# The sum of squares of the first norm: from eight TensorE products to GpSimd adds, with ScalarE's squares moved behind its rounding

## The reference, cut to what matters

```python
def rms_norm(x, g):
    xf = x.astype(jnp.float32)
    y = xf * lax.rsqrt(jnp.mean(xf * xf, axis=-1, keepdims=True) + EPS)
    return (y * g.astype(jnp.float32)).astype(x.dtype)

def diff_attention_layer(x, norm_g, w_in, ...):
    h = rms_norm(x, norm_g)
    q, k, v, z = jnp.split(h @ w_in, 4, axis=-1)
    q = rms_norm(q.reshape(b, s, DA_HEADS, 2, DA_HEAD), q_norm_g) * (DA_HEAD ** -0.5)
    ...
    return x + o @ w_out
```

## Time and profile before

| | |
|---|---|
| median of 3 runs | 1898.15 us (1897.22 to 1900.37) |
| span of the profiled execution, first to last instruction | 1896.2 us |
| TensorE products busy | 1868.0 us, 99% of the span |
| VectorE / ScalarE / GpSimd busy | 53% / 43% / 7% |
| mean granted TensorE clock | 0.998 of full speed |

### The profile page before, as it was taken

The page is one execution under the profiler, slowest core; times in us unless marked ns, Lnnn a source line. Parts: engine busy times, 40 slices in busy tenths (PEclk is TensorE's granted clock), DMA queues, the critical chain, the costliest instruction groups (busy, mean ns, idle before and its releaser), DMA issues.

```text
span 1896.2 us, 22387 instructions
## 1 busy us (share of the span) xinstructions
PE 1868.0 (99%) x8923; PEld 1450.5 (76%) x8923; DVE 996.8 (53%) x1778; ACT 817.9 (43%) x1328; POOL 123.8 (7%) x148
## 2 busy tenths in 40 slices
PE   8999999999999999999999999999999999999997
PEld 6566666666788788888886777778888878888886
DVE  6667666666544653333346667845434763333322
ACT  6566656656633342222323655434432442222221
POOL 0111111110001000000010011000000100000000
PEclk9999999999999999999999999999999999999999
DMA  5444343432233232222333323221123323233331
GB/s 199 164 145 156 144 145 145 145 145 101 78 129 117 67 111 100 93 96 94 100 86 125 99 70 106 68 94 35 45 89 111 124 92 102 94 100 97 92 95 61
DMA packets 56526, 201.95 MB, mean 107 GB/s; under 512 B 6478, under 2 KB 6934, under 8 KB 55784
## 3 DMA queue, kind: packets, MB, share of 16 engines
q1 hardware_dynamic: 44616, 158.32, 25.3%
q0 software_dynamic: 11808, 42.21, 6.1%
HBM read 195.23 MB, written 5.28 MB: 106 GB/s over the span
## 4 chain that ended last, share of the span: by engine, by line
PE 87%; DVE 6%; ACT 4%; issue 1%; DMA 0%; SPq 0%; DVEq 0%; ACTq 0%
PE ps L1204 25%; PE ps L1207 24%; PE ps L1205 24%; PE ps L1304 2%; PE ps L1268 2%; PE ps L1340 1%; ACT wH L1910 1%; PE ps L1292 1%; DVE wL L1499 1%; PE ps L1280 1%; ACT a L2009 1%; DVE a L1622 1%; PE ps L1347 1%; PE ps L1257 1%; DVE g1a L1499 1%
## 5 line engine op out<-in xcount | busy, mean ns | idle before, releaser
L1204 PE MATMUL ps<-hH,wH 128*128 128x512 f32 (+1 forms) x1560 | 634.8, 407 | 1.0 <-DVE hL L1570 1.0
L1207 PE MATMUL ps<-hH,wL 128*128 128x512 f32 (+1 forms) x1560 | 610.7, 391 | 1.0 <-DVE wL L1499 0.7
L1205 PE MATMUL ps<-hL,wH 128*128 128x512 f32 (+1 forms) x1560 | 609.0, 390 | 0.0
L1499 DVE TENSOR_TENSOR wL<-wr,wH 128x1024 fp32r<-128x1024 f32 (+2 forms) x285 | 343.9, 1207 | 483.8 <-ACT wH L1910 483.2
L1910 ACT ACTIVATE wH<-wr 128x1024 fp32r<-128x1024 f32 (+2 forms) x285 | 295.1, 1036 | 233.3 <-PE ps L1207 218.3
L1204 PEld LDWEIGHTS ps<-hH,wH 128*128 128x128 f32 (+1 forms) x1560 | 292.7, 188 | 93.6 <-issue 32.4
L1207 PEld LDWEIGHTS ps<-hH,wL 128*128 128x128 f32 (+1 forms) x1560 | 292.3, 187 | 66.9 <-DVE wL L1499 3.9
L1205 PEld LDWEIGHTS ps<-hL,wH 128*128 128x128 f32 (+1 forms) x1560 | 293.1, 188 | 61.3 <-issue 6.5
L1204 PE MATMUL ps<-gffn,wH 128*128 128x512 f32 x400 | 157.0, 393 | 1.0 <-DVE xT L1677 0.9
L1205 PE MATMUL ps<-gffn,wH 128*128 128x512 f32 x400 | 155.8, 390 | 0.0
L1207 PE MATMUL ps<-gffn,wL 128*128 128x512 f32 x400 | 155.8, 390 | 0.0
(11 more groups left out here) (304 smaller groups left out, 2079.9 us busy)
## 6 DMA issues: line engine op xcount, KB each, us to landing
wr<-wst SPq DMA_DIRECT2D x268, 512.0 KB, 3.4
a<-wfd POOLq DMA_DIRECT2D x54, 512.0 KB, 5.0
xT<-wfd POOLq DMA_DIRECT2D x18, 512.0 KB, 6.9
wr<-wst SPq DMA_DIRECT2D x16, 384.0 KB, 3.0
xT<-xin SPq DMA_DIRECT2D x8, 256.0 KB, 6.8
xT<-xin SPq DMA_DIRECT2D x2, 1024.0 KB, 7.0
xsave<-xT SPq DMA_DIRECT2D x1, 2048.0 KB, 7.3
c<-wfd POOLq DMA_DIRECT2D x8, 256.0 KB, 3.7
```

What stands on the lines that cost most here:

```text
L1204: e.matmul(o, hi, xh[k], start=k == 0, stop=False)
L1205: e.matmul(o, hi, xl[k], start=False, stop=False)
L1207: i = e.matmul(o, lo, xh[k], start=False, stop=k == t.nk - 1)
L1499: e.tensor_tensor(dst, x, hi.bitcast(F32), ALU.subtract).then_inc(s[name], 1)
```

## The change

Only the norm of x at the start is touched. The squares of x now go the way of the other norms: GpSimd adds chunks 0 to 6 into a buffer that nothing else uses at that time (`Vn[0]`), and TensorE sums two operands. The steps of the start are put in another order: all eight raw steps come first, with weight split 0 behind the first; then split 1; squares 0 to 3; split 2; squares 4 to 6; and square 7, at which TensorE does its two sums, stands between the fourth and the fifth chunk product of tv. Squares 4 to 7 wait for the add that has read their buffer.

```diff
-        self.add("norm_rs", n=n, stat=8 + 2 * n, rs=rs)
+        self.add("norm_rs", n=n, stat=2 + 2 * n, rs=rs)
...
         d.update(n=n, c=c, nsq=self.sig("nsq"))
-        if n == 0:
-            free = ("stat", self.sig("stat"))
-            d["stats"] = [free[1]]
-        elif c == 7:
+        if c == 7:
...
-        def chunk(c):
-            self.raw(0, c)
-            free[c % 4] = self.square(0, c, v=("first", c % 4), free=free[c % 4])
+        def square(c):
+            free[c % 4] = self.square(0, c, v=("first", c % 4), free=free[c % 4], acc_free=("rs", 0))
...
-        chunk(0)
-        chunk(1)
+        self.raw(0, 0)
         self.add("split", j=0)
-        mm(tq, 0, 1)
-        chunk(2)
-        chunk(3)
+        for c in range(1, 8):
+            self.raw(0, c)
+        mm(tq, *range(8))
         self.add("split", j=1)
-        mm(tq, 2, 3)
-        for c in range(4, 8):
-            chunk(c)
+        for c in range(4):
+            square(c)
         self.add("split", j=2)
-        mm(tq, 4, 5, 6, 7)
         mm(tk, *range(8))
-        mm(tv, *range(8))
+        for c in range(4, 7):
+            square(c)
+        mm(tv, 0, 1, 2, 3)
+        square(7)
+        mm(tv, 4, 5, 6, 7)
         rs = self.sig("rs")
-        self.add("norm_rs", n=0, stat=8, rs=rs)
+        self.add("norm_rs", n=0, stat=2, rs=rs)
...
-            return {1: acc1, 2: ff[0]["tmp"][0], 3: tq[0], 4: ff[1]["tmp"][0]}[n]
+            return {0: Vn[0], 1: acc1, 2: ff[0]["tmp"][0], 3: tq[0], 4: ff[1]["tmp"][0]}[n]
...
                 elif what == "square":
-                    if d["n"] == 0:
+                    if d["c"] == 7:
                         w.wait_ge(s["first"], 16)
-                        w.wait_ge(s["nsq"], d["nsq"])
-                        e.matmul(ps[7][:], C("one1024"), square_view(d), start=d["c"] == 0, stop=d["c"] == 7).then_inc(s["stat"], 1)
-                        bank_free[7] = ("rs", 1)
-                    elif d["c"] == 7:
                         take(7)
...
-                if what == "square" and d["n"] > 0:
+                if what == "square":
                     c, acc, v = d["c"], square_sum(d["n"]), square_view(d)
```

More of the change, by code:

```diff
@@ L256, in out_norm @@
     def out_norm(self):
-        self.add("norm", n=4, stat=16, rs=self.sig("rs"))
+        self.add("norm", n=4, stat=10, rs=self.sig("rs"))
     def chunks(self, n, c0, c1, rs, raw=None):
```

## The result

| | before | after |
|---|---|---|
| median of 6 runs each, compared in turn | 1899.84 us | 1906.33 us (1904.54 to 1908.17) |
| ratio | | 1.0039, interval 1.0029 to 1.0048 |
| span of the profiled execution | 1896.2 us | 1904.0 us |
| GpSimd busy | 7% | 7%, 8.7 us more |

What follows compares the result with a forecast made beforehand. The ScalarE and VectorE chain behind norm_rs's logarithm was taken as the bound; squares, adds and sums move that logarithm from 20.63 to 27.05, so 1898.15 + 6.4 = 1904.6 us, range 1902.0 to 1909.0.

Steps and rivals of the forecast that it cites:

- What bounds the kernel: From the logarithm at 20.63 to the scores, a ScalarE and VectorE chain; the end hangs on when `rs` exists.
- What is removed: At the start, six fewer square sums on TensorE, 5.2 us at full clock, counted as nothing because off the chain.
- Steps 1 and 2: Start: chunk 7 of x lands at 14.15; ScalarE then finishes square 1 at 16.85, and adds are asked at 16.95.
- Step 3: GpSimd's six dependent adds: 1.04 us alone, 1.15 behind a VectorE split, 0.10 to hand over; TensorE released at 25.07.
- adds at their recorded length: Rival on GpSimd's adds: six times 1.65 us from 16.95, logarithm at 28.83, +8.2, 1906.4 us; chance 0.17.
- the rival with the lost clock: Clock falls while TensorE waits for GpSimd; two sums at half speed add 1.72 us: 1906.3 us; chance 0.15.
- Steps 4 and 5: TensorE reaches the sums at 24.79, 0.3 us before GpSimd; two sums take 1.88, to 26.95; logarithm at 27.05.
- What is late next: After tq1, at about 35.1, TensorE idles; a fallen clock could lose up to 1.8 us, counted as nothing.
- The lock of VectorE and GpSimd: At the adds, a shared SBUF port pair held for whole instructions: +6.4 us by that rule, +6.1 without a lock.

Runs made afterwards that it cites:

- e2: The changed kernel's order on ScalarE and VectorE, but without GpSimd's adds: TensorE sums all eight squares directly behind the products of tq; 1902.06 us, ratio 1.0021.
- e3: The changed kernel with two more GpSimd adds ahead of the sixth, their results used by nothing; 1909.05 us, ratio 1.0056.
- e4: The changed kernel with TensorE's two sums moved ahead of all of tv, directly behind tk; 1907.01 us, ratio 1.0046.
- e5: The changed kernel with its six adds on VectorE instead of GpSimd and the two sums directly behind tk; 1901.62 us, ratio 1.0016.
- e6: The changed kernel with squares 4 to 7 before raws 4 to 7; GpSimd adds only squares 0 to 3, TensorE sums that and the rest; 1895.77 us.
- e1: The changed kernel with the old order (each chunk rounded, then squared), keeping GpSimd's six adds and TensorE's two sums; 1902.98 us, ratio 1.0024.
- e7: The changed kernel with squares 3 to 7 ahead of raws 4 to 7, TensorE summing all eight behind tq's first product, no GpSimd adds; 1897.10 us.

## Why the prediction was right, point by point

**What bounds the kernel: right.** "The end of the kernel hangs on when `rs` exists." In after, e2, e3, e4 and e5 the scores move by what the logarithm moves by, to 0.01 us, over a range of 7.8 us. In e6, with the logarithm moved the other way, it holds to 0.06. In e1 the scores lose another 0.3 and in e7 1.5, both times because ScalarE's next weight split waits for TensorE.

**What is removed, counted as nothing: right here.** 5.2 us of TensorE time went and the kernel got longer; e4 added 2.5 us of idle TensorE ahead of the sums at no cost to the scores of its profiled run. The saving has a value only where the squares come early and TensorE is late with tq, as in e7.

**Steps 1 and 2, x and ScalarE: right.** The first add was to start at 16.95 and started at 17.07: +0.12.

**Step 3, the adds: the term that was mis-sized.** "I take 1.04 alone and 1.15 behind a VectorE split, with 0.10 to hand over." Measured: 1.30 alone, 1.15 behind the split as said, 0.14 to hand over. The six were to take 8.02, to 24.97; they took 9.28, to 26.35: +1.26 of the +1.43 by which the logarithm was late (28.48 against 27.05). The collision with split 2 was placed right, on add 3. Four adds alone and five hand-overs make up 1.24 of it. What was wrong is the row for an add alone: the three instructions of 1.02 have `tiny` as their second operand (a multiplication by four columns, each spread over 128), and they do not wait for one another. e3's adds of two full operands that do not wait start 1.22 to 1.28 apart; whether the operation or the second operand makes the difference was not tried. A nearer row stood in the same group, the shortest add of `b`, 1372 ns, but it is no add alone either: in the trace of before it starts at 1492.45 under a VectorE split that ends at 1492.69, and ends 1.13 behind it. The estimate from the Trainium skill (GPSIMD Engine Reference, "Performance versus the Vector engine") of 1.12 was nearer to these 1.22 than my 1.04, and short of the 1.44 that an add costs in a chain.

The rival "adds at their recorded length" had the logarithm at 28.83 and the time at 1906.4: on the adds the truth, 9.28 for six or 1.55 a step, lies nearer to it (1.65) than to the forecast (8.02, or 1.34). It came near in size, not in its reason: the recorded 1.55 was taken to be an add alone, but an add alone is 1.30, and the rest came from one collision. The 1906.3 of the rival with the lost clock is met by the number alone: the sums took 2.0 at full clock.

**Steps 4 and 5, TensorE's arrival and the sums: right for the end.** TensorE reached the sums at 25.75, not 24.79, as it was still in tq when split 1's low part was ready; GpSimd was later still, so nothing came of it. The wait was 0.64 (0.3 forecast), the clock stayed full, and from the last add to the logarithm it took 2.13 (2.08 forecast).

**What is late next: half right.** TensorE was to be "done with tq1 at about 35.1". It did not begin it before 34.81: tq1 writes the bank that tq filled, and VectorE frees that only after `rs` (the 3.67-us wait for line 1524 above). Its weights, slot 3, are split behind `rs` too: ScalarE began at 31.86, VectorE ended at 34.16. I had let tq1 follow tv at once, and had followed neither its bank nor its weights. The clock did fall there, and again behind the wait of 46.13. Two stretches of after:

```profile
35.00:38.00 3.00, 3.00 (x8) 2.37 (x8) 2.44 (x5) 2.09 (x4) 0.00 (x0) 0.52 0.49 175
...
45.80:51.00 5.20, 4.87 (x12) 3.73 (x13) 4.97 (x8) 4.29 (x7) 1.99 (x4) 0.50 0.11 25
```

These are about 8 us at half speed, where up to 1.8 us of loss was feared; the cover named for it, the 2.19 us before the scores, was still 2.18. Counting it as nothing was right.

**The lock of VectorE and GpSimd (one waits until the other's instruction is through): right.** In after it shows on a split (1.88 against 1.23), an add (2.09 against 1.30) and a cast (1.31 against 0.22), and in e1 on five adds and seven VectorE instructions. The Trainium skill (SBUF — State Buffer, "SBUF: two separate sides") says that the shared port pair is held by one instruction for its whole length; the held-up ones here do end behind the holder, as that asks for: add 3 ends 1.15 behind split 2, the cast 0.08 behind add 3.

## What to carry to other kernels

In this kernel a step moved off the busiest engine gained only where that engine was late at the next point where the engines meet: ask of a shared result when it exists, not who is busy. Price a chain of dependent adds by the start-to-start time of dependent adds with two full operands, 1.44 us here on GpSimd, where VectorE did three in 2.27 to 2.49, and add a stretched instruction for each VectorE instruction of two inputs that it meets. The squares belong ahead of whatever nobody waits for, and GpSimd's share is what it can add before the last square arrives: that version runs 2.7 us faster than before.

## What the runs showed that was not expected

- The same two sums took 2.0 us in after and e4, and 3.6 to 3.8 in e3 and e1, at a granted clock of 0.53 and 0.50, after waits of 0.64, 3.14, 2.75 and 3.88 us. The length of the wait alone does not sort them, as e4's shows; what else differs was not tried.
- Even a small VectorE instruction takes part in the collision: the cast of 128x128, 0.22 alone, was held up for 1.1 us behind an add.
- The granted clock of 0.50 for some 8 us of the start left no mark on the scores; in e1 and e3 half that time, placed on the chain, did cost 1.6 to 1.8 us.
- In e1 and e2 the span grew 1.5 us more than the scores moved. That did not come from the start: GpSimd's add of 993.68 still stands 4.47 and 4.19 later than before, that of 1492.45 by 5.85 and 5.76. Between them, behind a wait of TensorE of 1.50 us that every kernel has there, e1 and e2 pass a stretch at a granted clock of 0.50, and before does not. Here are before, e1 and e2:

```profile
1286.00:1300.00 14.00, 13.30 (x196) 11.20 (x197) 7.36 (x11) 4.54 (x7) 0.00 (x0) 1.00 0.15 43
1294.00:1296.00 2.00, 2.00 (x5) 1.11 (x4) 0.00 (x0) 0.00 (x0) 0.00 (x0) 0.50 0.00 0
1292.00:1294.00 2.00, 2.00 (x22) 1.57 (x11) 1.37 (x2) 0.59 (x1) 0.00 (x0) 0.50 0.04 8
```

  The profiled runs of e1 and e2 were the longest of each kernel's (1904.29 and 1903.81). Whether the other runs of a kernel differ by the same stretch no trace shows.
